# The last step of the delta rule's triangular inverse on quarter tiles, TensorE's delta program written out, and VectorE's gram and tap work in another order

## The reference

```python
decay = jnp.where(lower, jnp.exp(jnp.where(lower, diff, 0.0)), 0.0)
kb = k * beta[..., None]
L = jnp.where(strict, jnp.einsum('bhnid,bhnjd->bhnij', kb, k) * decay, 0.0)
sol = lax.linalg.triangular_solve(L + jnp.eye(C, dtype=L.dtype), rhs, left_side=True,
                                  lower=True, unit_diagonal=True)
a_qk = jnp.where(lower, jnp.einsum('bhnid,bhnjd->bhnij', q, k) * decay, 0.0)
```

## Time and profile before

| | us |
|---|---|
| median of 3 runs | 2994.96 |
| lowest and highest | 2985.42, 2997.25 |
| the profiled execution's own time | 2996.62 |
| its span, first to last instruction | 2994.8 |
| TensorE busy in the span | 2867.1 |
| the delta iterations, first row sums to the output projection | 173.2 to 1111.3 |

### The profile page before, as it was taken

The page is one execution under the profiler, slowest core; times in us unless marked ns, Lnnn a source line. Parts: engine busy times, 40 slices in busy tenths (PEclk is TensorE's granted clock), DMA queues, the critical chain, the costliest instruction groups (busy, mean ns, idle before and its releaser), DMA issues.

```text
span 2994.8 us, 54254 instructions
## 1 busy us (share of the span) xinstructions
PE 2867.1 (96%) x21470; PEld 2685.3 (90%) x21470; DVE 1908.5 (64%) x2301; ACT 1219.6 (41%) x1503; POOL 826.8 (28%) x558
## 2 busy tenths in 40 slices
PE   6999999999999799999999999969999999999998
PEld 4789999999999687899999999969989988999996
DVE  1365656665666656765666566676798898644454
ACT  2344354454453434433333343334333333533343
POOL 1055565665565641000000000000455654000000
PEclk8999999999999899999999999989999999999999
DMA  9855655655555456666666666535545545555564
GB/s 365 299 163 188 202 161 172 208 172 181 190 184 176 141 190 204 204 187 186 185 185 186 186 183 187 183 126 165 159 147 162 164 148 164 176 184 184 181 203 148
DMA packets 283910, 552.56 MB, mean 185 GB/s; under 512 B 16817, under 2 KB 54258, under 8 KB 282610
## 3 DMA queue, kind: packets, MB, share of 16 engines
q1 hardware_dynamic: 263632, 474.02, 50.6%
q0 software_dynamic: 19408, 76.06, 6.8%
q10 hardware_dynamic: 722, 0.28, 0.0%
HBM read 548.19 MB, written 2.10 MB: 184 GB/s over the span
## 4 chain that ended last, share of the span: by engine, by line
PE 85%; DVE 9%; ACT 2%; issue 2%; DMA 1%; SPq 0%; DVEq 0%; POOL 0%; ACTq 0%; POOLq 0%; PEld 0%
PE pg L1030 33%; PE pg L786 16%; PE pd L1043 11%; PE pd L1030 7%; PE pg L1043 3%; PE pd L919 3%; PE pd L932 2%; PE pd L711 2%; PE pg L807 1%; DVE wl L1911 1%; DMA arena<-in_x 1%; PE pd L878 1%; PE pd L884 1%; PE pd L786 1%; DVE arena L2190 1%
## 5 line engine op out<-in xcount | busy, mean ns | idle before, releaser
L1911 DVE TENSOR_TENSOR wl<-wr,wh 128x1024 fp32r<-128x1024 f32 x616 | 771.1, 1263 | 539.0 <-ACT wh L1465 537.4
L1465 ACT ACTIVATE wh<-wr 128x1024 fp32r<-128x1024 f32 x616 | 652.3, 1060 | 1017.2 <-PE pg L1030 651.8
L1030 PE MATMUL pg<-hh,wh 128*128 128x256 f32 x2944 | 836.9, 284 | 12.0 <-DVE wl L1911 8.0
L1030 PE MATMUL pg<-hl,wh 128*128 128x256 f32 x2944 | 832.9, 283 | 0.0
L1030 PE MATMUL pg<-hh,wl 128*128 128x256 f32 x2944 | 832.3, 283 | 0.0
L568 POOL TENSOR_TENSOR wl<-wr,wh 128x1024 fp32r<-128x1024 f32 x195 | 479.6, 2462 | 513.7 <-ACT wh L1290 513.1
L1030 PEld LDWEIGHTS pg<-hh,wh 128*128 128x128 f32 x2944 | 564.0, 192 | 26.0 <-DVE wl L1911 13.1
L1030 PEld LDWEIGHTS pg<-hl,wh 128*128 128x128 f32 x2944 | 564.1, 192 | 0.5
L1030 PEld LDWEIGHTS pg<-hh,wl 128*128 128x128 f32 x2944 | 564.2, 192 | 0.0
L786 PE MATMUL pg<-hh,wh 128*128 128x256 f32 x1472 | 433.9, 295 | 1.1 <-ACT arena L1338 1.1
L1290 ACT ACTIVATE wh<-wr 128x1024 fp32r<-128x1024 f32 x216 | 227.5, 1056 | 477.7 <-PE pg L786 398.4
(11 more groups left out here) (362 smaller groups left out, 4507.8 us busy)
## 6 DMA issues: line engine op xcount, KB each, us to landing
wr<-in_w_in SPq DMA_DIRECT2D x224, 512.0 KB, 4.0
wr<-in_ffn_w_gu SPq DMA_DIRECT2D x176, 512.0 KB, 4.2
wr<-in_gdn_w_in SPq DMA_DIRECT2D x128, 512.0 KB, 4.0
arena<-in_mod_w POOLq DMA_DIRECT2D x64, 1024.0 KB, 6.8
wr<-in_ffn_w_down SPq DMA_DIRECT2D x88, 512.0 KB, 4.5
arena<-in_mod_w SPq DMA_DIRECT2D x32, 1024.0 KB, 12.2
wr<-in_gdn_w_in SPq DMA_DIRECT2D x128, 256.0 KB, 2.9
wr<-in_gdn_w_out SPq DMA_DIRECT2D x56, 512.0 KB, 4.5
```

The source lines that it names most:

```text
L1030: m = nc.tensor.matmul(bank[:, n * T:(n + 1) * T], w[s][:, k, n * P:(n + 1) * P], act[x][:, k0 + k, :], skip_group_check=True, start=(firs ...
L1465: a(wh[c % 4][:], wraw[c % 4], ACT.Copy).then_inc(s_hc, 1)
L1911: v.tensor_tensor(wl[c % 4][:], wraw[c % 4], wh[c % 4][:].bitcast(F32), ALU.subtract).then_inc(s_lc, 1)
```

## The change

The change has five parts.

1. At level 64, the two products use only the quarter that is not zero: 64 x 64 operands in place of 128 x 128, and VectorE's two operations behind them work on that quarter only (the first is now a copy, with no mask).
2. TensorE's loop over iterations 0 to 5 becomes a Python loop, so that the code of each iteration is written out.
3. The decay factors times the strict mask (into `Tb`) are made before the gram products are waited for; U is then made from the gram products directly, ahead of `lTb`, and no longer from `lTb`. The counters `u2` and `lt` change places.
4. `taps` moves from before the row factors to behind them, and the counter `scal` with it.
5. `mods` runs one step later: nothing at step 0, the two halves of tile 0 at step 1 (it was one half of tile 1 there), and so on to step 15 (it was 14).

```diff
--- before.py
+++ after.py
@@ -51,7 +51,7 @@
 PEO = order("ssq", "rows", "vtok", "gram", "ktok", "t2", "x2", "tx2", "u2", "x4", "tx4", "u4", "x8",
             "tx8", "u8", "x16", "tx16", "u16", "x32", "tx32", "u32", "x64", "ux64", "v0", "s", "o0", "r",
             "qs", "v1", "o1", "mod", "otr")
-VO = order("scal", "qkn", "dt", "lt", "u2", "at", *[f"{a}{s}" for s in LEVELS for a in ("x", "t")],
+VO = order("qkn", "dt", "scal", "u2", "lt", "at", *[f"{a}{s}" for s in LEVELS for a in ("x", "t")],
            "x64", "u64", "o0", "rhs1", "o1", "on", "modt", "og")
 AO = order("rn", "exp", "vtok", "kg", "t2", *[f"u{s}" for s in LEVELS], "v0", "s", "qs", "v1",
            "rstd", "qkv", "z")
@@ -916,8 +916,12 @@
 
                 def x_step(s):
                     for n in range(8):
-                        m = nc.tensor.matmul(pd[par][:, n * P:(n + 1) * P], lTb[:, n, :], Tb[:, n, :],
-                                             start=True, stop=True)
+                        if s == 64:
+                            m = nc.tensor.matmul(pd[par][64:P, n * P:n * P + 64], lTb[0:64, n, 64:P], Tb[0:64, n, 0:64],
+                                                 start=True, stop=True)
+                        else:
+                            m = nc.tensor.matmul(pd[par][:, n * P:(n + 1) * P], lTb[:, n, :], Tb[:, n, :],
+                                                 start=True, stop=True)
                     m.then_inc(s_pe, 1)
                 V("at")
                 Ac("t2")
@@ -945,7 +949,7 @@
                 Ac("u32")
                 par ^= 1
                 for n in range(8):
-                    m = nc.tensor.matmul(pd[par][:, n * P:(n + 1) * P], Xb[:, n, :], Ub[:, n, :],
+                    m = nc.tensor.matmul(pd[par][0:64, n * P + 64:(n + 1) * P], Xb[64:P, n, 0:64], Ub[64:P, n, 64:P],
                                          start=True, stop=True)
                 m.then_inc(s_pe, 1)
                 assert par == 0
@@ -1012,7 +1016,7 @@
                     pass
 
             gchunk(1, 0)
-            with pe.Fori(0, NIT - 2) as j:
+            for j in range(NIT - 2):
                 beside(delta(j), lambda c: gchunk(j + 1, c))
                 gchunk(j + 2, 0)
             beside(delta(NIT - 2), lambda c: gchunk(NIT - 1, c))
@@ -1794,10 +1798,6 @@
                 fq = qk.rearrange("p a b -> p (a b)")
                 v.tensor_tensor(sqb, fq, fq, ALU.mult).then_inc(s_sq1, 1)
                 link(v.tensor_copy(tkc, tk[:, :, bass.ds(it * VH, VH)]))
-                if mods:
-                    done(taps(it + 1))
-                else:
-                    dve.sem_inc(s_v, 1)
                 Ac("rn")
                 done(v.tensor_tensor(qk.rearrange("p a b -> p (a b)"), qk.rearrange("p a b -> p (a b)"), rnb, ALU.mult))
                 PEw("rows")
@@ -1807,18 +1807,28 @@
                         m = stt(out=dTb[:, n, :], in0=pd[1][:, n * P:(n + 1) * P], scalar=tkc[:, c, h:h + 1], in1=mneg[:],
                                 op0=ALU.subtract, op1=ALU.min)
                 done(m)
-                yield
+                if mods:
+                    done(taps(it + 1))
+                else:
+                    dve.wait_ge(s_v, bv + VO["dt"])
+                    dve.sem_inc(s_v, 1)
+                yield
+                Ac("exp")
+                link(v.tensor_tensor(Tb, dTb, bc_heads(m1t), ALU.mult))
                 PEw("gram")
-                Ac("exp")
+                for c in range(TT):
+                    for h in range(VH):
+                        n, b = c * VH + h, c * 2 + h // 2
+                        m = stt(out=Ub[:, n, :], in0=pd[0][:, b * P:(b + 1) * P], scalar=tkc[:, 2 + c, h:h + 1],
+                                in1=Tb[:, n, :], op0=ALU.mult, op1=ALU.mult)
+                link(m)
+                done(v.tensor_tensor(Ub, bc_heads(ident), Ub, ALU.subtract))
                 for c in range(TT):
                     for h in range(VH):
                         n, b = c * VH + h, c * 2 + h // 2
                         m = stt(out=lTb[:, n, :], in0=pd[0][:, b * P:(b + 1) * P], scalar=tkc[:, 2 + c, h:h + 1],
                                 in1=dTb[:, n, :], op0=ALU.mult, op1=ALU.mult)
                 done(m)
-                dve.wait_ge(s_v, bv + VO["lt"])
-                link(v.tensor_tensor(Ub, lTb, bc_heads(m1t), ALU.mult))
-                done(v.tensor_tensor(Ub, bc_heads(ident), Ub, ALU.subtract))
                 for b in range(4):
                     m = v.tensor_tensor(aTb[:, 2 * b:2 * b + 2, :],
                                         pd[0][:, 512 + b * P:512 + (b + 1) * P].unsqueeze(1).broadcast_to([P, 2, P]),
@@ -1826,7 +1836,7 @@
                 done(m)
                 yield
                 par = 0
-                Xf, Tf, Uf = (b.rearrange("p a b -> p (a b)") for b in (Xb, Tb, Ub))
+                Tf = Tb.rearrange("p a b -> p (a b)")
                 for s in LEVELS:
                     PEw(f"x{s}")
                     done(v.tensor_tensor(Xb, pd[par][:].rearrange("p (a b) -> p a b", b=P), bc_heads(msk[s]), ALU.mult))
@@ -1840,10 +1850,11 @@
                     par ^= 1
                     yield
                 PEw("x64")
-                done(v.tensor_tensor(Xb, pd[par][:].rearrange("p (a b) -> p a b", b=P), bc_heads(msk[64]), ALU.mult))
+                done(v.tensor_copy(Xb[64:P, :, 0:64], pd[par][64:P].rearrange("p (a b) -> p a b", b=P)[:, :, 0:64]))
                 yield
                 PEw("ux64")
-                done(v.tensor_tensor(Uf, Uf, pd[0][:], ALU.subtract))
+                done(v.tensor_tensor(Ub[0:64, :, 64:P], Ub[0:64, :, 64:P],
+                                     pd[0][0:64].rearrange("p (a b) -> p a b", b=P)[:, :, 64:P], ALU.subtract))
                 yield
                 PEw("o0")
                 done(v.tensor_copy(ob[:, 0:VH, :].rearrange("p a b -> p (a b)"), pd[0][:, 512:1024]))
@@ -1883,10 +1894,10 @@
 
             def mods(base, t):
 
-                if t == 0:
+                if t == 1:
                     mod_half(base, 0, 0)
-                if t < 15:
-                    mod_half(base, (t + 1) // 2, (t + 1) % 2)
+                if 1 <= t < 16:
+                    mod_half(base, t // 2, t % 2)
 
             with dve.Fori(0, NIT - 1) as j:
                 steps = delta(j, True)
```

## The result

The changed kernel takes 3001.39 us (median of 18 runs, 2998.57 to 3008.59), the kernel before 2990.82 beside it (18 runs): a ratio of 1.0037, 95% interval 1.0028 to 1.0046, so it is slower by 0.4%. I had said 2988, a touch faster. That was 6.8 us taken off the median of three runs, 2994.96; off the 2990.82 of the eighteen it would have been 2984. The profiled execution took 3000.43 us, with a span of 2998.6.

A forecast was written before the change was run, and what follows sets the result against it. TensorE was taken as the bound, busy 111.4 of 113.6 us a delta iteration. Terms -9.6 - 9.4 - 7 - 3.8 - 4 + 14 + 13 = -6.8 us gave 2988 us, with an 8-in-10 range of 2958 to 3014.

The forecast's parts named there:

- Part 1: Prediction's first term, TensorE's delta loop written out: five entry gaps shrink, slow stretches go, longer code costs nothing; -9.6 and -9.4 us.
- Loop gaps: TensorE's delta loop entries, before line 878: five gaps, 10.9 us in all, become five of 0.25 us; 9.6 us saved.
- Slow stretches behind them: Delta iterations from 406.6 and 751.8: two half-clock stretches behind loop gaps go too, 2 x 4.7 = 9.4 us saved.
- The quarter: Level 64 on 64 x 64 operands: 0.45 us saved in each of 16 steps, 7 us; gaining nothing had chance 0.1.
- Early U: U made from the gram products: its late arrival in iteration 6 and a slow stretch go, 3.8 us saved.
- Taps: VectorE's tap copies moved behind the row factors, where VectorE idles: no cost, no gain.
- The wait at chunk 7: TensorE waits 2.0 us for GpSimd's low part, queued behind tile 2's load, in seven iterations: +14 us; not coming, 0.2.
- Clock behind it: Clock lost after the seven chunk 7 waits, 1.85 us each on average: +13 us; clock holding, 2975 us, chance 0.15.
- Iteration 7: VectorE's first mask no longer holds TensorE up 5.7 us, chunk 7 waits some 3.7: 4 us saved, between 0 and 9.
- The shut-out: Rival: GpSimd's four lows in a row hold VectorE, T late for the transposes; 14 us, 3002 to 3015, chance 0.2.

The follow-up runs named there:

- the run above: Changed kernel with 156 idle instructions added to TensorE's stream ahead of the second block's mix loop: 2984.39 us, ratio 0.9974.
- The second trace with that stage: Trace of the kernel before with 102 idle instructions added ahead of the mix loop: its delta stage took 931.2 us; the kernel measured 3005.83 us, ratio 1.004.
- the shifts by 102, 156 and 256 instructions: Idle TensorE instructions ahead of the mix loop: 102 on the kernel before, 3005.83 us; on the changed kernel, 156 gave 2984.39 us and 256 gave 3004.11 us.

## Why the prediction was wrong

**The direction: one sentence failed.** Part 1 said "For longer code I charge nothing", and looked for a cost of fetching only in the straight code that was new. That code ran without an issue gap, as predicted. The cost came over 1000 us later, in a loop that no line of the diff touches: it was moved by part of a block, no longer stays on the chip, and fetches at each back edge. Price 13 us by the rows and the traces, 12 to 19 by the kernels. With it taken away the changed kernel has a ratio of 0.9974, 7.8 us faster than the kernel before, against the 6.8 that I had forecast.

I had the clue in hand: the issue gaps of the delta loop are the same thing. From 406.60 to 524.90 the kernel before has this row; its delta body is 7.5 blocks by the count (8.40 to 15.93) and touches eight, and it fetches in every iteration:

```profile
q8 instruction: 10, 0.16, 0.6%
```

I took that gap as the price of a branch, when it is the price of a loop whose code does not stay: the mix loop has the same kind of branch, and in the kernel before no wait behind it is put down to issue.

**The delta stage, term by term.** Forecast -6.8 us; measured -11.3 in the one pair of traces, -5 by the means of five, -7.8 by the ratio of the run above. In the pair TensorE's busy time is 18.9 us shorter (908.95 to 890.08), its idle time 7.6 longer.

- *Loop gaps*, -9.6: right. The five gaps of 10.9 us are gone and the entries wait some 0.24 each.
- *Slow stretches behind them*, -9.4: right as far as the trace goes; the two of 10.2 us did not come back, and cost half their length, 10.2. The second trace with that stage has one of 10.2 and one of 3.4.
- *The quarter*, -7: right, 7 to 9 by two pairs of kernels.
- *Early U*, -3.8: right for this change, no wait for U is left. The run with the loop alone shows what I did not say: without part 3, part 1 would have exposed it in all eight iterations (15.8 us).
- *Taps*, 0: no cost was seen in the changed kernel; not tried by itself.
- *The wait at chunk 7*, +14: right in place, cause and count, 16.3 us in seven waits. That it costs time was shown by moving the load that waits: -23 with what hangs on it.
- *Clock behind it*, +13: mis-sized by half. Four of the seven waits were followed by a slow stretch, of 3.4 us and not 10.2, which is 4 x 1.7 = 6.8 us. The 1.85 that I took as an average came from the longer stretches behind the loop's gaps.
- *Iteration 7*, -4: right within the scatter. Its first mask is no longer waited for (5.7 us before, 2.8 in the second trace), and its chunk 7 waits 3.6 us where I had said 3.7. From its row sums to the output projection it takes 114.4 to 116.8 us in three traces, and took 120.1 and 115.9 in two.
- *The shut-out*, a rival at 0.2 with 14 us and clock: it came in three of seven iterations here, for 5.8 us, and in five in another trace. I had it as a rival with its own chance, added to the clock; the runs show the two as alternatives, one or the other in each iteration. So 6.8 + 5.8 = 12.6 us is what stands where I had +13, and that this agrees is luck.

No rival held a cost outside the stage. The measured time, 3001.39, lies in the range, but by luck: it is the sum of a stage about as forecast and a cost from elsewhere, not of anything that the range was made from.

## What to carry to other kernels

Look at the instruction queue in the view of the DMA queues before a loop is written out or lengthened: packets that recur in every pass, with an issue wait at the first instruction behind the back edge, mean a loop whose code does not stay on the chip, and any edit ahead of another loop of nearly that length can push it over the same edge. Compare the windows of what was not edited first; a cost there is about placement, and some idle instructions in a hole before the loop test it and mend it. When an operation is moved, ask which queue stands still for it: here the same reordering was worth +8.5 us or -14 (2992.85 to 3001.39 or to 2978.55), by the place of one DMA issue on GpSimd.

## What the hardware showed beyond that

- A loop of some 6.7 blocks of 16 KB was fetched once when it lay in seven blocks, and in nine packets a pass when it touched eight; the wait behind its back edge was then 2.2 to 3.2 us, and 1.9 to 2.4 in the delta loop before. That eight is the edge rests on my count of the compiled program, and on the shifts by 102, 156 and 256 instructions.
- Consecutive lows of GpSimd kept VectorE out for their whole run: two operations of 0.8 us took 7.08 us beside three lows and 9.63 beside four. With the lows spaced out, the same two took 3.52. An operation that reads PSUM and one SBUF tensor, line 1842, was not held up (1.23 us inside a run of lows).
- An idle stretch of 2.3 us was followed by half clock in four cases of seven, for 3.4 us; those behind the delta loop's gaps before lasted 10.2. Where the clock held, a late T took its place, so that iterations at either clock lasted nearly the same (114.5 to 114.7 us at the lower, 115.3 to 115.5 at full clock). What decides between the two clocks these runs don't show.
